# A three-phase transformer kernel: the first phase's weight ring gets seven buffers that are split in place

## The reference

```
first_block:
  h = rms_norm(x, attn_norm);  proj = h @ w_in            # q_f k_f v_f f_logit q_s k_s v_s gl_f gl_s
  o_f = fox_attention(8 heads, with a cumulative forget term)
  o_s = swa_sink_attention(8 heads on 2 kv heads, window 128, rotary)
  x  += (sigmoid(gl_f) * (o_f @ w_proj_fox) + sigmoid(gl_s) * (o_s @ w_proj_swa)) @ w_out
  h = rms_norm(x, ffn_norm);  top 1 of 8 groups, top 2 of its 8 experts
  x  += sum of gate * (silu(h @ w1[e]) * (h @ w3[e])) @ w2[e]        # 64 experts, w1 w3 w2: 2 MB each
  x   = rms_norm(x, final_norm)
second_block, two layers:
  layer 0: gMLP mixing and attention into 256 memory tokens;  layer 1: MoBA and memory attention
  each: x = layer_norm(ALPHA*x + mix @ w_mix_out);  x = layer_norm(ALPHA*x + swiglu(x))
```

## Time and profile before

| | |
|---|---|
| three runs | 1710.25, 1712.14, 1712.56 us; median 1712.14 |
| profiled execution, its span (first to last instruction) | 1709.9 us; no other time is given for it |
| PE, PE weight load, DVE, ACT busy | 1344.7, 916.5, 617.3, 418.7 us |
| bytes moved, DMA queue 1 | 538.76 MB, 79.6% of 16 engines' span |
| first expert matmul | 207.27 us |
| last wait for an expert chunk ends | 1124.7 us |

### The profile page before, as it was taken

How to read it: one execution, slowest core, us unless ns; L and a number is a source line. 1 busy time by engine, 2 the same in 40 slices (tenths; PEclk the granted TensorE clock), 3 DMA queues, 4 the chain that set the end, 5 groups by cost and what they waited for, 6 DMA issues and landing times.

```text
span 1709.9 us, 20307 instructions
## 1 busy us (share of the span) xinstructions
PE 1344.7 (79%) x8918; PEld 916.5 (54%) x8918; DVE 617.3 (36%) x821; ACT 418.7 (24%) x569; POOL 10.0 (1%) x64
## 2 busy tenths in 40 slices
PE   8999877686655656565665556689999999999998
PEld 8999724142212212221221222159888889898886
DVE  5667401001100100110011001047866676776665
ACT  5754400000000000000000000045544435444441
POOL 2000000000000000000000000000000000000000
PEclk9999989888877887877887878789999999999999
DMA  9545899999999999999999999994556655345560
GB/s 297 182 158 206 343 418 427 429 426 428 426 428 429 427 428 427 428 428 428 427 428 425 426 428 426 421 306 162 199 174 196 210 184 173 106 166 177 192 213 34
DMA packets 132233, 540.07 MB, mean 316 GB/s; under 512 B 8528, under 2 KB 90800, under 8 KB 108080
## 3 DMA queue, kind: packets, MB, share of 16 engines
q1 hardware_dynamic: 132128, 538.76, 79.6%
q10 hardware_dynamic: 16, 0.00, 0.0%
HBM read 537.69 MB, written 1.05 MB: 315 GB/s over the span
## 4 chain that ended last, share of the span: by engine, by line
PE 51%; DMA 36%; DVE 5%; ACT 4%; SPq 3%; issue 2%; DVEq 0%; ACTq 0%
DMA big<-in_w_dram 35%; PE bank L1768 9%; PE bank L2101 8%; PE bank L104 7%; PE bank L106 7%; PE bank L105 7%; PE bank L1797 4%; PE bank L2102 4%; SPq L95 3%; ACT hi_b L321 1%; DVE lo_b L335 1%; PE bank L1113 1%; PE bank L592 1%; PE bank L555 1%; PE bank L1730 1%
## 5 line engine op out<-in xcount | busy, mean ns | idle before, releaser
L1768 PE MATMUL bank<-big,xe 128*32 128x512 f32 x1984 | 284.4, 737 | 251.6 <-DMA big<-in_w_dram 251.6
L1768 PEld LDWEIGHTS bank<-big,xe 128*32 128x32 f32 x1984 | 78.1, 132 | 456.0 <-issue 456.0
L335 DVE TENSOR_TENSOR lo_b<-raw_b,hi_b 128x2048 fp32r<-128x2048 f32 x90 | 205.6, 2291 | 105.9 <-ACT hi_b L321 105.9
L1860 DVE TENSOR_TENSOR x<-bank,x 128x512 f32<-128x512 f32 x60 | 41.5, 692 | 530.1 <-PE bank L1712 530.1
L2101 PE MATMUL bank<-xT,hi_b 128*128 128x512 f32 x576 | 204.3, 398 | 0.0
L321 ACT CAST hi_b<-raw_b 128x2048 fp32r<-128x2048 f32 x91 | 172.8, 1904 | 20.4 <-PE bank L106 20.4
L1797 PE MATMUL bank<-big,gT 128*32 128x512 f32 x936 | 132.2, 716 | 54.7 <-DMA big<-in_w_dram 54.7
L2102 PE MATMUL bank<-xT,lo_b 128*128 128x256 f32 x576 | 161.7, 281 | 0.0
L2101 PEld LDWEIGHTS bank<-xT,hi_b 128*128 128x128 f32 x576 | 108.2, 188 | 26.4
L1797 PEld LDWEIGHTS bank<-big,gT 128*32 128x32 f32 x936 | 36.6, 128 | 135.9 <-issue 135.9
L2102 PEld LDWEIGHTS bank<-xT,lo_b 128*128 128x128 f32 x576 | 108.8, 189 | 0.6
(11 more groups left out here) (338 smaller groups left out, 2174.6 us busy)
## 6 DMA issues: line engine op xcount, KB each, us to landing
big<-in_w_dram SPq DMA_DIRECT2D x190, 2048.0 KB, 20.5
raw_b<-in_w_ffn_in_dram SPq DMA_DIRECT2D x44, 1024.0 KB, 5.1
raw_b<-in_w_ffn_out_dram SPq DMA_DIRECT2D x22, 1024.0 KB, 5.1
raw<-in_w_in_dram SPq DMA_DIRECT2D x15, 1024.0 KB, 9.9
raw_b<-in_b_w_in_dram SPq DMA_DIRECT2D x10, 1024.0 KB, 5.1
raw_b<-in_w_mix_out_dram SPq DMA_DIRECT2D x8, 1024.0 KB, 5.1
raw_b<-in_a_w_in_dram SPq DMA_DIRECT2D x7, 1024.0 KB, 12.8
raw<-in_w_out_dram SPq DMA_DIRECT2D x4, 1024.0 KB, 5.1
```

The lines of the kernel that those rows point to most:

```text
L335: dve.tensor_tensor(self.lo[i % NRAW], self.raw[i % NRAW], self.hi[i % NH].bitcast(F32), ALU.subtract).then_inc(*self.s_lo.up(i))
L1768: last = pe.matmul(hb.t[32 * e:32 * e + 32, :], xe[:, k, 32 * e:32 * e + 32], each[e][k // 4][:, k % 4 * 512:(k % 4 + 1) * 512], start=(k ...
```

## The change

The first phase's ring gets seven buffers instead of six. `lo` is written over `raw`, so the three `lo` buffers go, and the ring moves up to start at column 4096, behind slot 1's place. A load into the ring waits for PE's use of the chunk seven back instead of the split of the chunk six back. Slot 1 shares no column with the ring, so `free(1)` waits for nothing. `free` now looks at seven ring buffers and three `hi` buffers, and waits for uses by PE alone; slot 2's waits for `mT` go. The slots are loaded in the order 3, 2, 4 to 7. The attentions of the third phase share the semaphores of the first phase's, counted on from where those end.

As `for i in range(1, NR)` in `sp_first` loads the rest of the ring before the small loads, chunk 6 now stands ahead of them.

```
-NR = 6
+NR = 7
...
     def load(self, sp, i):
         if i >= NR and i - NR >= self.split:
-            sp.wait_ge(*self.s_lo.of(i - NR))
+            sp.wait_ge(*self.s_used.of(i - NR))
...
-            dve.tensor_tensor(self.lo_[i % NB][:, 0:k], self.raw_[self.slot(i)][:, 0:k],
+            dve.tensor_tensor(self.lo_[self.slot(i)][:, 0:k], self.raw_[self.slot(i)][:, 0:k],
                               self.hi_[i % NB][:, 0:k].bitcast(F32), ALU.subtract).then_inc(*self.s_lo.up(i))
...
-        return view(self.hi_[i % NB]), view(self.lo_[i % NB]), i
+        return view(self.hi_[i % NB]), view(self.lo_[self.slot(i)]), i
...
-    m.raw = [region(f"raw{i}", CHUNK) for i in range(NR)]
+    m.raw = [region(f"raw{i}", CHUNK, SLOT + i * CHUNK) for i in range(NR)]
+    m.lo = [region(f"lo{i}", CHUNK, SLOT + i * CHUNK, F32R) for i in range(NR)]
     m.hi = [region(f"hi{i}", CHUNK, None, F32R) for i in range(NB)]
-    m.lo = [region(f"lo{i}", CHUNK, None, F32R) for i in range(NB)]
-    m.free = m.top
+    m.free = 12 * CHUNK
+    assert m.top <= m.free
...
-            for k in range(NR + 2 * NB):
-                if k * CHUNK < hi and (k + 1) * CHUNK > lo:
-                    if k < NR:
-                        sp.wait_ge(*s["lo"].of(max(c for c in range(n) if self.w_a.slot(c) == k)))
-                    else:
-                        sp.wait_ge(*s["used"].of(max(c for c in range(n) if c % NB == (k - NR) % NB)))
+            for k in range(NR + NB):
+                if SLOT + k * CHUNK < hi and SLOT + (k + 1) * CHUNK > lo and lo < m.free:
+                    last = [c for c in range(n) if (self.w_a.slot(c) == k if k < NR else c % NB == k - NR)]
+                    sp.wait_ge(*s["used"].of(max(last)))
             if i == 2:
                 sp.wait_ge(*s["used"].of("gated"))
-                sp.wait_ge(*s["mT_hi"].of("all"))
-                sp.wait_ge(*s["mT"].of("all"))
...
-        for i in range(2, NS):
+        for i in (3, 2, *range(4, NS)):
             free(i)
             self.load_m(sp, i)
...
-        self.mem0 = Attention(s, "_b", buf, mem_jobs(0), 0, 0)
+        self.mem0 = Attention(s, buf, mem_jobs(0), self.mix.end, self.mix.n_out)
```

More of the change, by code:

```diff
@@ L271, in lower_first @@
         k = self.half(h)
-        dve.tensor_tensor(self.lo_[0][:, k], self.raw_[self.slot(0)][:, k], self.hi_[0][:, k].bitcast(F32),
+        dve.tensor_tensor(self.lo_[self.slot(0)][:, k], self.raw_[self.slot(0)][:, k], self.hi_[0][:, k].bitcast(F32),
                           ALU.subtract).then_inc(*self.s_lo.up((0, h), *([0] if h else [])))
@@ L505, with __init__ @@
 class Attention:
-    def __init__(self, s, tag, buf, jobs, base, n_out, hold=0, late=0):
+    def __init__(self, s, buf, jobs, base, n_out, hold=0, late=0):
         self.jobs, self.base, self.hold, self.late = jobs, base, hold, late
@@ L518, in __init__ @@
         (self.s_score, self.s_masked, self.s_peak, self.s_exps, self.s_p_turned, self.s_p_out, self.s_value,
-         self.s_o_out, self.s_o_turned, self.s_o_hi, self.s_o_lo) = (s[n + tag] for n in (
+         self.s_o_out, self.s_o_turned, self.s_o_hi, self.s_o_lo) = (s[n] for n in (
              "score", "masked", "peak", "exps", "p_turned", "p_out", "value", "o_out", "o_turned", "o_hi", "o_lo"))
@@ L757, in first_plan @@
                      sinks=self.sinkb) for qt in range(2)]
-        self.mix = Attention(s, "", (m.pb_a, m.ptb_a, m.osb_a), jobs, 0, 0, hold=11, late=1)
+        self.mix = Attention(s, (m.pb_a, m.ptb_a, m.osb_a), jobs, 0, 0, hold=11, late=1)
         self.mix.s_sink = s["sink"]
@@ L1969, in last_plan @@
         buf = (m.pb_b, m.ptb_b, m.osb_b)
-        self.mem0 = Attention(s, "_b", buf, mem_jobs(0), 0, 0)
+        self.mem0 = Attention(s, buf, mem_jobs(0), self.mix.end, self.mix.n_out)
         jobs = mem_jobs(1) + [j for i in range(3) for j in moba_jobs(i)]
-        self.moba = Attention(s, "_b", buf, jobs, self.mem0.end, self.mem0.n_out)
+        self.moba = Attention(s, buf, jobs, self.mem0.end, self.mem0.n_out)
     def sp_last(self):
@@ L2225, in pe_last @@
         banks, cat = {}, pair(m.catT)
-        onto(banks, cat, ("mix", 0), 6, True, lambda c, t: [(s["o_lo_b"], ("mem01", 0))])
+        onto(banks, cat, ("mix", 0), 6, True, lambda c, t: [(s["o_lo"], ("mem01", 0))])
         tail(1, banks, ("mix", 0), [(cat, c0, lambda c, t: [(s["mixed"], ("lo", c // 2))]) for c0 in (0, 2, 4)])[1]()
@@ L2233, in outs @@
         def outs(c, t):
-            return [(s["o_lo_b"], (f"moba{c // 2}{t}" if c < 6 else f"mem1{t}", 0))]
+            return [(s["o_lo"], (f"moba{c // 2}{t}" if c < 6 else f"mem1{t}", 0))]
         fill = {4 * i + 2 * k: [lambda i=i, name=name: across((name, 1, i), ev, 2)]
```

## The result

The changed kernel takes 1716.76 us (median of 8 runs, 1714.32 to 1717.69). The kernel before takes 1712.35 beside it. One of that kernel's eight runs took 1863.18 us; the ratio is of the others, whose median is 1712.14. The ratio is 1.0024, 95% interval 1.0014 to 1.0033: slower by about 4.4 us (4.1 by the ratio). 1716.2 was forecast, from a range of 1711.8 to 1718.5.

What follows compares the result with a forecast made beforehand. It took the kernel as bound by PE waiting for expert weights, their stream pinned to PE's release of slot 1. Stall 2.9 + clock 1.4 - slots 0.2 = +4.1 us on 1712.14: 1716.2 us, range 1711.8 to 1718.5.

Steps and rivals of the forecast that it cites:

- The seventh load ahead of the small ones: At the start, chunk 6 ahead of the vrow loads makes PE stand 3.2 us instead of 0.3: +2.9 us.
- the sum: Whole kernel: 2.9 stall + 1.4 clock - 0.2 earlier slots = +4.1 us, giving 1716.2 us.
- The clock: After PE's break at vrow, the clock falls from 2.4 to 1.2 GHz, costing +1.4 us, with 0 as other bound.
- Rival A: At the vrow break, PE stalls but the clock does not fall: +2.9 - 0.2, 1714.8 us; chance 0.2.
- Nothing gives it back: From 26 to 207 us the chain names no DMA, so the 2.9 us stall is not recovered later.
- In-place split, later releases, shared semaphores: In the ring and attentions, these parts cost zero; the semaphores at most 0.1 us, taken as none.
- Rival D: In the first phase's ring, one late release holds SP's loads, costing some 5 us more, 1721; chance 0.04.
- Earlier slots: Expert slots fill DMA holes before 209 us, but the stream is pinned to slot 1's release: gain 0.2 us.
- rival B: At the expert stream's start, bytes and not slot 1's release set it: 3.9 us earlier, about 1712.3; chance 0.12.
- bound of 0.7: Most the expert stream gains from slot 1's reload: 10.3 us before, against 9.6 for the load at 136.99.
- The clock's luck elsewhere: The clock's fall at 203.3 us may go away or come again: 1.4 us either way, put in the range.
- Rival E: The clock's luck elsewhere: fall at 203.3 us may vanish or recur, 1.4 us either way; chance not given separately.

Runs made afterwards that it cites:

- e1: Changed kernel with chunk 6 loaded behind the small loads again, all else kept: 1711.71 us, ratio 1.0004 to the kernel before.
- e2: Kernel before, six buffers, with only chunk 6's load moved ahead of the small loads: 1716.99 us, ratio 1.0033.
- e3: Changed kernel, load order kept, PE transposing vrow behind k1 and DVE copying it behind chunk 5's split: 1709.48 us, ratio 0.9987.
- e11: Changed kernel with 13 unread matmuls in PE's break ahead of vrow's transpose: 1714.27 us, ratio 1.0015.
- e5: e1 with slots 5 to 7 held until PE has turned the memory tokens: 1714.87 us, ratio 1.0021.
- e8: Kernel before (old ring) with e3's edit, vrow transposed behind k1: 1709.64 us, ratio 0.9988.
- e4: e1 with expert slots held back and ordered as in the kernel before: 1712.10 us, ratio 1.0004.
- e10: e6 with 9 unread matmuls ahead of the norm's transposes: 1707.79 us, ratio 0.9976.
- e6: e3 with 28 unread identity matmuls in PE's idle time round the routing: 1708.22 us, ratio 0.9982.
- e7: e6 with 19 unread matmuls ahead of the norm's transposes: 1709.15 us, ratio 0.9985.
- e9: e8 with e6's 28 unread matmuls round the routing: 1708.70 us, ratio 0.9982.

## Why the prediction was right, point by point

*The seventh load ahead of the small ones.* Right in place, a little low in size. The turn of `vrow` moved by 3.54 us, 25.26 to 28.80. Of these, 2.92 are the later issue, just as forecast, and 0.62 a longer way to landing, which the sum had put at nothing. PE's own stand grew by 3.1 us only, since in this execution PE came 0.4 us later to it. e1, e2 and e3 show it from three sides: undone, alone, and with the order kept but PE's wait moved.

*The clock.* Right. It fell at 29.7 for 3.4 us. From the transpose to the end of k0 went 7.58 us instead of 6.09, 1.5 where 1.4 was forecast, and e11 took just that away. The clock fell at PE's breaks of e2 (5.0 us) and e5 (2.5 us) too. Rival A, a stall without the fall, did not happen.

*Nothing gives it back.* Right. `sel` begins 5.05 us later: 3.5 at `vrow` and 1.5 behind it. What PE came later to `vrow` (0.4) is inside the 3.5, for PE waits there anyway.

*In-place split, later releases, shared semaphores.* No cost that can be told from nothing, as said: e1, and e8 with e3. The split takes 2292 ns. Chunk 24 is issued at 153.26 and cast only at 182.66, and no cast of the first phase waits for a load behind 30 us. Rival D did not come up.

*Earlier slots.* Right that the stream is pinned to slot 1's release, and rival B, the backlog, is refuted by e1 and e4. The bound of 0.7 was badly founded. The load at 136.99 was not alone: a 1 MB load issued at 136.58 took 4.8 us to land and was still under way. And the trace of before had shorter ones, 8.3 us for the load at 175.21 and 7.5 for the one at 192.20:

```profile
136.58 0.37 SPq L95 DMA_DIRECT2D raw<-in_w_out_dram  x1
136.99 0.47 SPq L95 DMA_DIRECT2D big<-in_w_dram  x1
...
DMA to landing us min/median/max: 8.3/8.3/8.3
...
DMA to landing us min/median/max: 7.5/7.5/7.5
```

In the changed kernel slot 1's reload took 9.0 us instead of 10.3, 1.3 less, where 0.2 was forecast. Whether the early slots did that is not shown: with the slots as late as before it took 9.0 in e4 and 9.1 in e2 as well, and 11.2 in e8. In the medians there is no gain that can be told from nothing: e1 and e4 are alike, and so are e3 and e8.

*The clock's luck elsewhere.* Rival E, which I had put in the range alone, is the rest of the profiled difference. From PE's first expert matmul to the release of slot 1 went 8.08 us instead of 5.82, 2.3 more at the low clock, and from `sel` to that matmul 0.4 more. The marks then add up: 5.05 + 0.4 + 2.3 - 1.3 = 6.4 at the landing of slot 1's reload, measured 6.41. The last phase was 0.9 shorter in this execution (from the last `big` to the end 583.8 to 585.3 us pass in the thirteen profiled executions, so this is within their spread), which leaves the 5.6 of the spans. The medians differ by 4.4; only one execution of each kernel has marks, so how much of this luck the other runs had is not shown.

The forecast of 4.1 us was thus close in its two large terms. That the median came within 0.6 us of the forecast is in part luck: `vrow` cost 0.6 more than forecast, the reload's landing 1.1 less, and how often the low clock meets the first expert matmuls lay outside the sum. The marks of the profiled execution show it: the first expert matmul came at 212.70 and the release of slot 1 at 220.78, where 211 and 217.2 were written. One reading beside the sum was off too: of the 2.2 us "around the span", some 1.2 are (1716.75 against 1715.5 for the changed kernel's profiled run); the rest is that the profiled execution of before was shorter than the median. The sum does not rest on it.

Open: what sets a reload's 7.4 to 11.2 us behind an emptied queue; what e3 and e8 gained beyond the 0.3 us that PE stood in the profile of before; and e10's step over e6, which is too small for the runs made.

## What to carry to other kernels

When a transfer phase is bound by bytes, look for the one issue from which it runs without a hole, and ask what releases it: here PE's second quarter of work, so filling idle DMA ahead of it bought nothing that could be measured, while late loads cost 3 us (e5). A change of a ring's size also changes what a loop that fills the ring puts ahead of the small loads behind it. A small operand that is wanted late must not be turned by an engine in its busiest line: moving the reader by two chunks was worth more than the whole new ring.

## What the runs showed of the hardware that I had not expected

The full clock of PE came at 10.1 to 16.5 us in kernels that are alike at the start, and it alone sets whether q1 ends at 23.8 (e2) or 25.5 (e1). A wait for a DMA behind it hides this luck: in the changed kernel and e2 `vrow` was turned at 28.80 and 28.82 in both cases. The low stretch round the routing lay anywhere from 3.4 (before) over 6.8 (e4) to 10.2 us (changed), or was missing (e1). With some 28 matmuls whose results nobody reads it was missing in all four profiled executions that have them (e6, e7, e9, e10), against one of nine without. And slot 1's 2 MB reload, released when the older loads had landed and only the half of slot 0 was still under way, took from 7.4 (e6) over 9.0 (e4, changed) to 11.2 us (e8). What lies ahead on the queue does not explain that spread.
